# Two input chunks and four weight pieces moved into the opening stage of a two-block transformer kernel

## The reference

```python
h = rmsnorm(x, norm_gain[l]) * (1.0 + scale[:, None, :]) + shift[:, None, :]
proj = h @ w_in[l]
```

## Time and profile before

| | |
|---|---|
| median of 3 runs | 3205.55 us (3204.19 to 3206.41) |
| profiled execution, its own time | 3203.59 us |
| its span (first to last instruction) | 3201.7 us |
| PE busy | 2155.5 us, 67% |
| DVE busy | 1710.8 us, 53% |
| ACT busy | 869.0 us, 27% |
| POOL busy | 794.7 us, 25% |
| mean granted TensorE clock | 0.838 |
| chain that ended last, by engine | PE 54%, DMA 30%, DVE 9%, ACT 3% |

### The profile page before, as it was taken

One profiled execution on the slowest core, in us unless ns is written; L12 is line 12 of the kernel. 1 busy time (PEld: TensorE's weight loads), 2 busy tenths in 40 slices (PEclk: granted clock), 3 DMA queues, 4 the chain that ended last, 5 costly groups with the idle time before them and its releaser, 6 DMA issues.

```text
span 3201.7 us, 30897 instructions
## 1 busy us (share of the span) xinstructions
PE 2155.5 (67%) x12338; PEld 1479.8 (46%) x12338; DVE 1710.8 (53%) x2746; ACT 869.0 (27%) x1327; POOL 794.7 (25%) x680
## 2 busy tenths in 40 slices
PE   5899999989998999999989981222323233222235
PEld 2676777877787777666668871000000000000001
DVE  3436556554656654343445689556555655565430
ACT  1333444444454444553535420000000000000000
POOL 1111100000000000000000025555555555555552
PEclk8999999999999999999989995666666666666667
DMA  9898864557754545343325687999999999999998
GB/s 385 286 299 282 280 198 148 184 177 246 220 170 137 165 143 162 106 138 99 118 76 170 212 311 304 421 421 422 421 421 422 421 421 422 422 420 422 422 422 339
DMA packets 243594, 901.01 MB, mean 281 GB/s; under 512 B 20374, under 2 KB 45228, under 8 KB 177004
## 3 DMA queue, kind: packets, MB, share of 16 engines
q0 software_dynamic: 94208, 612.85, 47.6%
q1 hardware_dynamic: 148768, 285.58, 27.6%
q10 hardware_dynamic: 476, 0.62, 0.1%
HBM read 894.78 MB, written 2.10 MB: 280 GB/s over the span
## 4 chain that ended last, share of the span: by engine, by line
PE 54%; DMA 30%; DVE 9%; ACT 3%; issue 2%; POOL 1%; SPq 0%; DVEq 0%; ACTq 0%; POOLq 0%
PE pp L1718 47%; DMA late<-in_peer_v,MI 10%; PE tp L1718 6%; DMA P<-in_peer_v,MI 5%; DMA ring<-in_peer_v,MI 5%; DMA x<-in_peer_v,MI 4%; DVE wL L1067 2%; DMA SY<-in_peer_v,MI 2%; PE tp L1721 2%; DMA late<-in_w_mod 2%; ACT wH L583 1%; DMA ring<-in_peer_w_query 1%; DMA ring<-in_w_in 1%; DMA SY<-in_w_mod 1%; DVE P L1677 0%
## 5 line engine op out<-in xcount | busy, mean ns | idle before, releaser
L1067 DVE TENSOR_TENSOR wL<-ring,wH 128x1024 fp32r<-128x1024 f32 (+3 forms) x504 | 582.2, 1161 | 598.3 <-ACT wH L583 594.9
L1718 PE MATMUL pp<-wH,hH 128*128 128x512 f32 (+3 forms) x1888 | 749.0, 397 | 38.9 <-DVE wL L1067 28.5
L1718 PE MATMUL pp<-wH,hL 128*128 128x512 f32 (+3 forms) x1888 | 717.5, 380 | 0.0
L1718 PE MATMUL pp<-wL,hH 128*128 128x512 f32 (+3 forms) x1888 | 717.1, 380 | 0.0
L583 ACT ACTIVATE wH<-ring 128x1024 fp32r<-128x1024 f32 (+3 forms) x504 | 505.4, 1008 | 473.3 <-PE pp L1718 316.5
L1718 PEld LDWEIGHTS pp<-wH,hH 128*128 128x128 f32 x1888 | 359.2, 190 | 182.5 <-issue 71.0
L1718 PE MATMUL pp<-late,S 128*32 128x512 f32 x736 | 227.3, 874 | 296.0 <-DMA P<-in_peer_v,MI 75.7
L1718 PEld LDWEIGHTS pp<-wH,hL 128*128 128x128 f32 x1888 | 358.4, 190 | 63.8
L1718 PEld LDWEIGHTS pp<-wL,hH 128*128 128x128 f32 x1888 | 359.8, 191 | 55.8 <-issue 1.2
L1718 PE MATMUL pp<-P,S 128*32 128x512 f32 x376 | 269.6, 885 | 151.6 <-DMA x<-in_peer_v,MI 75.8
L1718 PE MATMUL pp<-x,S 128*32 128x512 f32 x376 | 166.5, 880 | 223.1 <-DMA ring<-in_peer_v,MI 223.1
(11 more groups left out here) (302 smaller groups left out, 3005.7 us busy)
## 6 DMA issues: line engine op xcount, KB each, us to landing
ring<-in_w_in SPq DMA_DIRECT2D x288, 512.0 KB, 4.4
ring<-in_w_out SPq DMA_DIRECT2D x96, 512.0 KB, 4.4
P<-in_w_mod POOLq DMA_DIRECT2D x85, 512.0 KB, 5.0
late<-in_w_mod SPq DMA_DIRECT2D x64, 512.0 KB, 9.1
SY<-in_w_mod POOLq DMA_DIRECT2D x43, 512.0 KB, 5.3
ring<-in_w_in SPq DMA_DIRECT2D x48, 368.0 KB, 4.2
ring<-in_peer_w_query SPq DMA_DIRECT2D x32, 512.0 KB, 5.0
ring<-in_w_in SPq DMA_DIRECT2D x24, 344.0 KB, 3.2
```

The costliest lines, as they stand in the source:

```text
L1067: tt(lo, raw, hi.bitcast(F32), ALU.subtract).then_inc(*tick("dve_lo", *names))
L1718: return e.matmul(o, l, r, start=start, stop=stop, skip_group_check=skip)
```

## The change

The order of the column blocks becomes 0, 2, 1, 3, so that shift and scale of the first half of the 2048 rows of `h` are there after 32 products; `chunk 0, 0` and `chunk 0, 1` wait only for these. The slots of the first 64 loads move out of `late` (to `TAB` and `P`), so that `hH`, `hL`, `wH` and `wL` can be written meanwhile. SP issues load m+7 at step m of lane M rather than all at the front of its queue, so other loads can stand between them. The steps of X stand at k = 20 to 43. Splits of pieces 0 to 2 stand after k = 34, chunk 0 after k = 36, chunk 1 after k = 38, and pieces 0 to 3, each with the splits up to three ahead, after k = 47, 51, 55 and 59. Chunks 2 and 3 both stand ahead of piece 4. `project` passes over the first four pieces, with their pumps.

```diff
+            if p == 0 and q < 4:
+                continue
             yield from splits(p, q)
             if p in (0, 2) and n == 0:
-                for c in {0: (0, 1), 2: (2,), 4: (3,)}.get(pc, ()):
+                for c in ({0: (0, 1), 2: (2,), 4: (3,)} if p else {4: (2, 3)}).get(pc, ()):
                     yield "chunk", p, c
...
     for k in range(64):
         yield "step", "M"
-        if k >= 20 and k % 2:
+        if 20 <= k < 44:
             yield "step", "X"
+        if k == 34:
+            yield from splits(0, 0)
+        if k in (36, 38):
+            yield "chunk", 0, k // 2 - 18
+        if k == 44:
+            yield "drain", "X"
+        if k in (47, 51, 55, 59):
+            q = (k - 47) // 4
+            yield from splits(0, q)
+            yield "piece", 0, q
+            yield from splits(0, q + 1)
     yield "step", "M"
-    yield "drain", "X"
-    yield "split", 0, 0
-    yield "split", 0, 1
-    asked[0] = 2
...
-        mod_in = [*[late[:, 1024 * b:1024 * b + 1024] for b in range(8)], P[:, 0, GA:GA + 1024], P[:, 1, GA:GA + 1024],
+        mod_in = [*[TAB[:, 1024 * b:1024 * b + 1024] for b in range(4)],
+                  *[P[:, t, c:c + 1024] for t in range(2) for c in (4160, 5184)], P[:, 0, GA:GA + 1024], P[:, 1, GA:GA + 1024],
...
+        def first_mods(m):
+            return range(8) if m == 0 else range(m + 7, min(m + 8, 64))
+        def mod_block(block):
+            return (0, 2, 1, 3, 4, 5)[block] if block < 6 else block - 6
...
+                for m in range(16 * b0, 16 * b1):
+                    for j in first_mods(m) if b0 == 0 else ():
+                        c0, k = mod_block(j // 16) * 1024, j % 16
+                        b, before = mod_slot(j)
                         if before is not None:
                             w.wait_ge(*at("mod used", before))
...
-                    w.wait_ge(*at("mods", 9 if p else 3))
+                    w.wait_ge(*at("mods", 9 if p else (1, 3)[c // 2]))
```

More of the change, by code:

```diff
@@ L528, in mods @@
             def mods(b0, b1):
[L529 to L532, removed]
+                for m in range(16 * b0, 16 * b1):
+                    for j in first_mods(m) if b0 == 0 else ():
+                        c0, k = mod_block(j // 16) * 1024, j % 16
+                        b, before = mod_slot(j)
                         if before is not None:
                             w.wait_ge(*at("mod used", before))
-                        e.dma_start(mod_in[b], I["w_mod"][0, k * 128:(k + 1) * 128, block * 1024:block * 1024 + 1024]).then_inc(
-                            *landed(f"mod_in{b}", ("mod", m)))
-                for m in range(16 * b0, 16 * b1):
+                        e.dma_start(mod_in[b], I["w_mod"][0, k * 128:(k + 1) * 128, c0:c0 + 1024]).then_inc(
+                            *landed(f"mod_in{b}", ("mod", j)))
                     yield
@@ L1215, in mods @@
                     u = next(turn)
-                    l, k0 = block // 6, block % 6 * 8
+                    l, k0 = block // 6, mod_block(block) * 8
                     mc = mcol[:, l, k0:k0 + 8]
@@ L1221, in mods @@
                         *tick("dve_side", ("pair free", u)))
-                    if block % 6 in (2, 3):
+                    if mod_block(block) in (2, 3):
                         w.wait_ge(*now("dve_side"))
```

## The result

The changed kernel is slower: 3216.2 us at the median of 8 runs (3209.87 to 3218.3) against 3205.24 us (8 runs, 3201.4 to 3207.46), a ratio of 1.0029 with a 95% interval of 1.0019 to 1.0040 (the ratio is estimated over the runs, and is not the quotient of the two medians, which is 1.0034). Forecast were 3203.5 us and a range from 3194.5 to 3208.5. The profiled execution took 3209.87 us, with a span of 3208.0; it is the shortest of the eight, and 6.3 us over the profiled execution of before. The kernel before moves by some us from session to session, so I compare ratios within a session, and spans only between profiles.

The account below looks back on a forecast made before the run. Transfers and PE were taken to hold the end by turns. A saves 15.9 us, B costs 5.65 and C 8.2: 2.0 us gained, 3203.5 us against the median, range 3194.5 to 3208.5.

Parts of the forecast that it names:

- B: Before load 63: six ring loads stand ahead of it in full DMA engines and delay product 63's end by 5.65 us.
- C: At k = 34 to 36: the fourth comparison tile waits behind splits, PE stands still, transfers run dry; costs 8.2 us.
- The first three are covered: Comparison tiles at k = 21, 26 and 31: eight loads in flight, 10.5 us, cover PE's waits; no cost taken.
- T: The end of product 63, at 97.23 us before; forecast to move 13.9 us later.
- A: After product 63: with pieces 0 to 3 and chunks 0 and 1 done, the end gets 15.9 us shorter; lower end 14.6.
- The sum: Whole kernel: product 63 ends 13.9 us later, what follows is 15.9 us shorter, so 2.0 us gained.
- PE stays at half clock: Rival, chance 0.07: clock 0.50 from 77 us to the end of group 0; 13.4 us lost, 3218.9 us.
- The passed-over pumps: After product 63: four pumps leave 0.48 over, so one product, not two, falls before piece 9; 0.54 us still owed.
- What comes after it I take to move with it: Everything after the start of piece 9 was taken to move with that start, T + 33.3 before, T + 16.9 forecast.

Follow-up runs that it names:

- tables_dense: order_only with the steps of X at k = 20 to 43, one for each k; 3205.22 us, ratio 1.0006 to the kernel before.
- tile_first: Changed kernel with the splits of pieces 0 to 2 after k = 36, behind the fourth comparison tile, not after k = 34; 3200.12 us, ratio 0.9993.
- early_prep: Changed kernel with the first table step at k = 8, splits of pieces 0 to 2 at k = 35, split of piece 6 behind chunk 2; ratio 0.9982.
- split6_late: Changed kernel with the split of piece 6 behind chunk 2 instead of behind piece 3; 3212.09 us, ratio 1.0031.
- filler: early_prep with 16 more transposes, without a use, behind those of chunk 3; 3197.47 us, ratio 0.9969.
- order_only: Changed kernel keeping only column-block order, slots and loads issued one by one; tables, chunks, pieces and pumps as before; 3202.92 us, ratio 0.9998.
- splits_alone: tables_dense with the splits of pieces 0 to 2 after k = 34, no chunk or piece beside the loads; 3215.81 us, ratio 1.0042.
- no_pieces: tile_first with pieces 0 to 3, their pumps and later splits left after product 63, chunk 2 ahead of piece 2; 3202.26 us, ratio 0.9995.
- pumps_back: early_prep with the pumps of pieces 0 to 3 put back; 3197.47 us, ratio 0.9976.

## Why the prediction was wrong

**B, more bytes ahead of load 63: right.** 5.65 us were forecast. From tables_dense to tile_first, which adds six ring loads and no hole, product 63 moves from 100.38 to 105.93, 5.55 us. The five kernels from early_prep on, with six ring loads, no hole and no long wait for the first tile, end it 4.8 to 5.5 us later than before. That the first difference meets the forecast to 0.1 us is luck, given how profiles scatter.

**C, the hole: the mechanism right, the size low.** I had 8.2 us, bounds 5.8 to 11.8. From tile_first to the changed kernel product 63 moves by 10.05 us, and by 12.0 in the second profile; alone it is 11.4. PE waits for the forecast reason (11.89 us, where about 10 were forecast), but the last split ends at 74.3 instead of 72.4, since the loads before it were already late, the transposes took 1.97 us (I took 1.5, the bound was twice 1.03), and the transfers then did not come back at once: 193 GB/s from 82 to 88 us, and a load issued at 85.88 landed after 5.28 us, where I took 3.4. The page "DMA: Bandwidth & Descriptors" of the Trainium skill, cited in C by its section "Anatomy of one DMA — SWDGE (gpsimd) path", has its formula, and so the estimate of 3.2 us, from loads that gpsimd issues; these loads are issued by SP, and the measured 5.28 decides. The lower bound of 5.8 also leaves out the 0.5 us that it names; by its own terms it is 6.3.

**"The first three are covered": wrong, 3.2 us.** This is the step that I had taken at nothing. I argued from the eight loads in flight, and from the DMA share of 1.03 in two waits of before. But the wait is 5.40 us, not 2.39, and nothing is issued in it, so it uses up most of that lead; and behind it a table step stands with every product, which I had priced at 0.54 + 0.76 = 1.30, full clock, though the row from 43 to 52 us said 0.50. It took 1.76 us against 1.31 of a load up to 53 us, and 1.27 after that, too little to fill the queue again soon. tables_dense measures 3.15 us, early_prep takes it away.

So T moves by 3.15 + 5.55 + 10.05 = 18.75 us instead of 13.9. That these add up exactly is no test of them, as they are steps between the same four profiles.

**A, the end after T: mis-sized, 12.3 us instead of 15.9.** Piece 9 starts 0.57 us after product 65, at 136.5 = T + 20.5, and not at T + 16.9. The term of 13.5 us from T to product 64 measured 17.15. Of the 3.65, 0.9 is the split of piece 6, which holds `msum`: I had moved it off the path in my reading, but it stands on ACT ahead of `msum`, and waits for ring load 6, which is issued behind load 63. Another 0.9 is the clock in the transposes of chunks 2 and 3 of that profile (split6_late is without both). In pieces 4 and 5 the clock costs 1.3 (filler), which I had named as a bound (14.6 instead of 15.9) and set to nothing "as PE was busier before". The remaining 0.5 I did not place. In the second profile of the changed kernel the whole is 2.65.

**The sum.** 12.3 - 18.75 is 6.5 us lost at piece 9, where 2.0 gained were forecast. Each of the four errors had the same sign, and in three of them one habit has a part: the half clock was put in the bound and full clock in the value. In the end after T it is the 1.3 and the slow transposes, in the hole some 0.5 (1.97 against 1.5), and of the thin queue the smaller part. The rival 'PE stays at half clock' had it too strong (13.4 us lost) but on the right side. It was given 0.07.

**The passed-over pumps: seen, but read too near.** The prediction counts them for products 64 to 66 and not for lane X, whose debt lasts to the end. With them passed over the expert stage is 1377.0 to 1378.6 us long in six profiles (the changed kernel twice, tile_first, split6_late, early_prep, filler), and 1372.0 to 1373.2 in the six with all of them (before, order_only, tables_dense, splits_alone, no_pieces, pumps_back). In the layers ahead of it the passed-over pumps give some us back, so that the sum by span hardly shows it: in the changed kernel 7.1 us between product 64 and 1829 us, then 5.3 lost.

**"What comes after it I take to move with it": wrong, though the sum hides it.** By profiles the differences of 8.1 and 9.1 us at product 64 shrink to 1.0 and 2.9 at the start of the expert stage and end as 6.3 and 7.0 in the span. That the 6.5 us lost at piece 9 and the 6.3 of the span agree is luck: most of the first was given back, and most of the second was made later, by the lane's debt. By ratio the whole is 9.3 us with an interval of some 3 us to either side, and the 11 us between the first session's medians and the 9 between the second's lie within it. Why the layers ahead of the expert stage give 7 us back with four pumps less was not tested further than pumps_back, where they do not.

## What to carry to other kernels

Where all engines walk one written order, a load and the work that waits for it are two placements: put the load early, and its first consumer behind everything on that engine that others wait for; here one moved line was worth 11 us of 3211. Before a wait of the engine that frees the load slots, count how many loads land while none is issued. Price the work after the wait at the clock that the rows show after such waits, as the value and not as a bound, and compare the issue interval of the loads that it gates with the time of a load. And when steps are paid out from a running debt, an edit at the front shifts them everywhere: look for the stage where that matters, or pay the debt back.

## What the runs showed of the hardware that was not expected

**A queue with loads outstanding ran below its rate.** In the changed kernel products 22 to 25 were about 1.76 us apart. By my count from the ends of products and the rates, about two or more loads of 512 KB were still to land all that time, and yet from 52 to 60 us 300 GB/s flowed (278 in tables_dense) where 408 did otherwise, and from 53 to 57 us 250, when a load was issued every 1.27 us. Why a queue that is not empty runs so low, no run here shows.

**The clock fell without a long idle gap.** In splits_alone PE was without work for 12.3 us, and the clock was 0.50 from 71 to 84 us. Then it was 1.00 from 85 to 94 us, and fell again: it stayed at 0.50 to the end of the loads, with 10.86 us of PE busy in the 13 from 100 to 113. These products take 1.08 us instead of 0.64, so the slow clock itself makes much of the busy share, and at 1.00 before (67 to 97 us) the share was 74%: the share of a stretch does not tell its clock. What stood ahead of the second fall was thin work, one product for each load and no table step or piece between. tables_dense shows it most plainly, where from 86 us to the fall near 95 PE was never idle for more than 0.67 us at a time:

```profile
92.11 0.64 PE L1726 MATMUL pp<-TAB,cact 128*32 128x256 f32 x8 [0.63 <-DMA TAB<-in_w_mod]
93.40 0.64 PE L1726 MATMUL pp<-TAB,cact 128*32 128x256 f32 x8 [0.65 <-DMA TAB<-in_w_mod]
94.68 1.04 PE L1726 MATMUL pp<-TAB,cact 128*32 128x256 f32 x8 [0.64 <-DMA TAB<-in_w_mod]
```

**A wait of 2 us was followed by a fall of the clock in the middle of dense work.** In the changed kernel PE was idle from 121.4 to 123.4, started piece 4 at full clock, and fell to 0.50 at 124.7 us for 3.4 us. The page "TensorE: Matmul & The Clock Gate" of the Trainium skill warns, in "Why this matters for your kernels", of long idle gaps between bursts of matmuls. This gap was 2.0 us, behind thin work and transposes at half clock; in split6_late it was 2.69 us, the transposes had run at full clock, and the clock fell at 123.1 all the same. In filler, with 0.95 us left of the gap, it stayed at 1.00. So shorter gaps than the page warns of mattered here; thin work stood ahead of them in all three, and no run takes it away.
